# The high weight of ffn1 meets both parts of the rows in three matmuls of 364, 362 and 362 columns instead of four of 272

## The reference

```python
h2 = _rmsnorm(x, P['norm_ffn'])
gt, up = jnp.split(h2 @ P['w_ffn_in'], 2, axis=-1)
x = x + ((jax.nn.silu(gt) * up) @ P['w_ffn_out']).astype(x.dtype)
```

## Time and profile before

| | |
|---|---|
| median of three runs | 3008.64 us (3006.72 to 3013.38) |
| profiled execution, span from first to last instruction | 3010.2 us |
| mean granted TensorE clock | 0.954 of full |
| PE busy / PEld busy | 2699.9 us (90%) / 2534.6 us (84%) |
| POOL, DVE, ACT busy | 1315.4, 1119.3, 665.0 us |
| matmuls (and as many weight loads) | 25812 |
| ffn1 with dense matmuls, each of the two layers | about 257.5 us |

### The profile page before, as it was taken

One profiled execution on the slowest core, in us unless ns is written; L12 is line 12 of the kernel. 1 busy time (PEld: TensorE's weight loads), 2 busy tenths in 40 slices (PEclk: granted clock), 3 DMA queues, 4 the chain that ended last, 5 costly groups with the idle time before them and its releaser, 6 DMA issues.

```text
span 3010.2 us, 66079 instructions
## 1 busy us (share of the span) xinstructions
PE 2699.9 (90%) x25812; PEld 2534.6 (84%) x25812; DVE 1119.3 (37%) x1758; ACT 665.0 (22%) x1156; POOL 1315.4 (44%) x1083
## 2 busy tenths in 40 slices
PE   5898988889899989999978889888889999899997
PEld 5887877777799989999977778777878999899997
DVE  4435254462411231115644552535534113211165
ACT  3223232232211121111232232313222111211122
POOL 4333242431365545555542422414324555455564
PEclk9999999999699999999989999999988999999998
DMA  5112021110122323222321111202011223232122
GB/s 174 40 48 64 20 75 41 41 54 25 60 84 84 102 82 91 85 75 73 101 91 35 56 50 35 77 23 70 26 45 65 84 84 119 69 91 84 62 80 84
DMA packets 70704, 206.66 MB, mean 69 GB/s; under 512 B 10640, under 2 KB 14752, under 8 KB 69488
## 3 DMA queue, kind: packets, MB, share of 16 engines
q1 hardware_dynamic: 59760, 175.03, 18.9%
q10 hardware_dynamic: 7200, 16.26, 1.4%
q0 software_dynamic: 3552, 12.56, 1.3%
HBM read 185.20 MB, written 18.61 MB: 68 GB/s over the span
## 4 chain that ended last, share of the span: by engine, by line
PE 64%; DVE 13%; PEld 11%; issue 5%; ACT 2%; POOL 2%; DMA 2%; DVEq 0%; SPq 0%; ACTq 0%; PEldq 0%; POOLq 0%
PE psP L591 31%; PE psQ L591 13%; PE psQ L654 9%; PEld psP L591 8%; DVE BIG L1365 7%; PEld psQ L591 3%; PE psQ L647 3%; PE psQ L930 1%; DVE BIG L1368 1%; POOL WS L453 1%; PE psP L920 1%; DMA BIG<-in_s_ret 1%; DVE UB L1365 1%; PE psP L654 1%; PE psP L914 1%
## 5 line engine op out<-in xcount | busy, mean ns | idle before, releaser
L591 PE MATMUL psP<-HH,WS 128*128 128x272 f32 x5728 | 1074.2, 299 | 60.5 <-DVE HL L1365 19.9
L591 PEld LDWEIGHTS psP<-HH,WS 128*128 128x128 f32 x5728 | 852.3, 193 | 93.9 <-issue 24.9
L451 POOL TENSOR_SCALAR WS<-W 128x512 fp32r<-128x512 f32 (+1 forms) x312 | 246.0, 788 | 1145.3 <-PEq L585 712.7
L453 POOL TENSOR_TENSOR WS<-W,WS 128x512 fp32r<-128x512 f32 (+1 forms) x312 | 508.8, 1631 | 26.0
L591 PE MATMUL psP<-HL,WS 128*128 128x272 f32 x1984 | 417.8, 293 | 0.0
L654 PE MATMUL psQ<-BIG 64*64 64x64 f32 (+1 forms) x5696 | 283.9, 235 | 60.9 <-DVE BIG L1365 25.2
L591 PE MATMUL psQ<-BIGR 128*128 128x272 f32 x2032 | 333.3, 287 | 0.0
L591 PEld LDWEIGHTS psP<-HL,WS 128*128 128x128 f32 x1984 | 320.1, 193 | 0.0
L654 PEld LDWEIGHTS psQ<-BIG 64*64 64x64 f32 x5696 | 223.2, 135 | 111.8 <-issue 95.5
L591 PE MATMUL psQ<-HH,BIGR 128*128 128x272 f32 x1760 | 304.5, 287 | 0.0
L453 POOL TENSOR_TENSOR BIGR<-W,BIGR 128x512 fp32r<-128x512 f32 (+1 forms) x160 | 293.1, 1832 | 13.4
(11 more groups left out here) (226 smaller groups left out, 3047.9 us busy)
## 6 DMA issues: line engine op xcount, KB each, us to landing
W<-in_w_stage SPq DMA_DIRECT2D x88, 512.0 KB, 3.6
W<-in_w_f SPq DMA_DIRECT2D x88, 512.0 KB, 3.6
W<-in_w_gate SPq DMA_DIRECT2D x48, 512.0 KB, 3.6
W<-in_w_f SPq DMA_DIRECT2D x88, 256.0 KB, 2.6
W<-in_w_br SPq DMA_DIRECT2D x48, 256.0 KB, 2.6
W<-in_w_out SPq DMA_DIRECT2D x16, 512.0 KB, 3.6
x_waiting<-X SPq DMA_DIRECT2D x4, 1088.0 KB, 8.0
X<-x_waiting ACTq DMA_DIRECT2D x2, 2176.0 KB, 9.9
```

The costliest lines, as they stand in the source:

```text
L451: pool.tensor_scalar(high, src, 1.0, 0.0, ALU.mult, ALU.add).then_inc(high_part[q], 1)
L453: pool.tensor_tensor(low, src, high, ALU.subtract).then_inc(split[q], 1)
L591: mm = pe.matmul(out[:, a, 0:HT], a_, x_[:, a * HT:(a + 1) * HT], start=(first and n == 0), stop=(last and n == 2))
```

## The change

Rows for ffn1 get a layout of their own, `H2`: 1088 columns for each of the 8 input blocks, high and low part side by side. Columns 0 to 363 are the 272 high columns of the first half and 92 low ones; columns 364 to 725 are the 272 high columns of the second half and 90 low ones; columns 726 to 1087 are the other 362 low ones. The high weight runs over the 1088 columns in three matmuls (364, 362, 362), and the low weight over the two groups of 272 high columns in two: 40 matmuls for a tile instead of 48.

A gate tile now uses P0 (two banks) and a bank of Q0, an up tile P1 and a bank of Q1. The low columns' products no longer add up in PSUM under the high ones: ScalarE copies them out of three places into a buffer (`low_part`, three ACTIVATEs), VectorE adds the PSUM's high part to it (`join`), and sigmoid and products work on that sum. VectorE writes the low rows of norm2 in four pieces instead of one (`low_wide`), and ScalarE's high rows go into two groups of 272. `H2` lies where `HL` and a free block before it lie; `HH` is not read by ffn1 any more. After ffn1 ScalarE waits until the last product is written (`f_done`).

Three semaphores of two recurrent branches become one each, with counted values; two helpers of VectorE become names for the engine's own calls. Neither changes an instruction that computes.

```diff
+W1, W2 = 364, 362
...
-    ("ffn1", FF_T // 2, [("g0", "P0"), ("u0", "Q0"), ("g1", "P1"), ("u1", "Q1")]),
+    ("ffn1", FF_T, [("g", "P0"), ("u", "P1")]),
...
                 def ffn1(i, first):
                     for t in range(2):
-                        project_split(l, "ffn1", i, f"g{t}", HH, HL, rows=ROWS["H2"] if first and t == 0 else None)
-                        project_split(l, "ffn1", i, f"u{t}", HH, HL)
...
+                        for n in "gu":
+                            use = f"{n}{t}"
+                            b = wait_free(pe, l, "ffn1", 2 * i + t, n)
+                            third = ps["Q0" if n == "g" else "Q1"][:, 0]
+                            q = weights_split(l, "ffn1", i, use)
+                            for k in range(KD):
+                                if first and t == 0 and n == "g":
+                                    pe.wait_ge(rows_split, l * ROWS_N + ROWS["H2"] + k + 1)
+                                high, low = (v[:, k * P:(k + 1) * P] for v in SW[q])
+                                pe.matmul(b[:, 0, 0:W1], high, H2[:, k, 0:W1], start=k == 0, stop=False, skip_group_check=True)
+                                pe.matmul(b[:, 1, 0:W2], high, H2[:, k, W1:W1 + W2], start=k == 0, stop=False,
+                                          skip_group_check=True)
+                                pe.matmul(third[:, 0:W2], high, H2[:, k, W1 + W2:2 * TOK], start=k == 0, stop=k == KD - 1)
+                                pe.matmul(b[:, 0, 0:HT], low, H2[:, k, 0:HT], start=False, stop=k == KD - 1, skip_group_check=True)
+                                mm = pe.matmul(b[:, 1, 0:HT], low, H2[:, k, W1:W1 + HT], start=False, stop=k == KD - 1,
+                                               skip_group_check=True)
+                                release()
+                            mm.then_inc(fullof("ffn1", n), 1)
...
+                def low_part(dst, b, third):
+
+                    act.activation(dst[:, 0:W2], third[:, 0:W2], ACT.Copy)
+                    act.activation(dst[:, W2:W2 + W1 - HT], b[:, 0, HT:W1], ACT.Copy)
+                    return act.activation(dst[:, W2 + W1 - HT:TOK], b[:, 1, HT:W2], ACT.Copy)
+
                 with act.Fori(0, FF_T // 2) as i:
                     for t in range(2):
...
+                        b = wait_full(act, l, "ffn1", n, "g")
+                        act.wait_ge(f_done, l * FF_T + n + 1)
+                        low_part(NT[t], b, ps["Q0"][:, 0]).then_inc(f_low, 1)
+                        wait_emptied(act, l, "ffn1", n, "g")
+                        act.activation(SQ[t], NT[t], ACT.Sigmoid).then_inc(f_sig, 1)
+                        b = wait_full(act, l, "ffn1", n, "u")
+                        act.wait_ge(f_gated, l * FF_T + n + 1)
+                        low_part(NT[t], b, ps["Q1"][:, 0]).then_inc(f_low, 1)
+
+                act.wait_ge(f_done, l * FF_T + FF_T + 2)
...
+            def low_wide(l, n, k, src):
+
+                dve.wait_ge(rows_high, l * ROWS_N + n + 1)
+                v = H2[:, k]
+                tt(v[:, W1 + W2:W1 + W2 + HT], src[:, 0:HT], v[:, 0:HT], ALU.subtract)
+                tt(v[:, W1 + W2 + HT:2 * TOK], src[:, HT:W2], v[:, W1:W1 + W2 - HT], ALU.subtract)
+                tt(v[:, HT:W1], src[:, W2:W1 + W2 - HT], v[:, W1 + W2 - HT:W1 + W1 + W2 - 2 * HT], ALU.subtract)
+                tt(v[:, W1 + HT:W1 + W2], src[:, W1 + W2 - HT:TOK], v[:, W1 + W1 + W2 - 2 * HT:W1 + HT],
+                   ALU.subtract).then_inc(rows_split, 1)
...
                 with dve.Fori(0, FF_T // 2) as i:
                     for t in range(2):
...
+                        b = wait_full(dve, l, "ffn1", n, "g")
+                        dve.wait_ge(f_low, 2 * (l * FF_T + n) + 1)
+                        join(NT[t], b).then_inc(emptyof("ffn1", "g"), 1)
+                        dve.wait_ge(f_sig, l * FF_T + n + 1)
+                        wait_emptied(dve, l, "ffn1", n, "g")
+                        tt(SQ[t], SQ[t], NT[t], ALU.mult).then_inc(f_gated, 1)
+                        b = wait_full(dve, l, "ffn1", n, "u")
+                        dve.wait_ge(f_low, 2 * (l * FF_T + n) + 2)
+                        join(NT[t], b).then_inc(emptyof("ffn1", "u"), 1)
+                        wait_emptied(dve, l, "ffn1", n, "u")
+                        tt(FF[:, bass.ds(n, 1)], SQ[t].unsqueeze(1), NT[t].unsqueeze(1), ALU.mult).then_inc(f_done, 1)
+                        dve.wait_ge(f_done, l * FF_T + n + 3)
```

More of the change, by code:

```diff
@@ L150 @@
  sdec um vm A_sq A_rstd A_n A_y2 A_o
- B_g B_c0 B_c1 B_q B_k B_qd B_vm B_s1_ B_s2_ B_s3_ B_sq B_rstd B_n B_o
- C_g C_f0 C_f C_k0 C_qp C_tot C_vm C_s1_ C_s2_ C_s3_ C_dk C_sq C_rstd C_n C_o C_lvl C_add""".split()
+ B_g B_c0 B_c1 B_q B_k B_qd B_vm B_s B_sq B_rstd B_n B_o
+ C_g C_f0 C_f C_k0 C_qp C_tot C_vm C_s C_dk C_sq C_rstd C_n C_o C_lvl C_add""".split()
 def trunk(nc, A, OUT, XD):
@@ L283, in trunk @@
         M = blocks(BIG[:, 2 * ON:2 * ON + KD * TOK], TOK)
+        H2 = blocks(BIGR[:, at_r[0]:at_r[0] + 2 * KD * TOK], 2 * TOK)
         at_r[0] += KD * TOK
@@ L321, in trunk @@
         x_ready, f_sig = sem("x_updated"), sem("f_sigmoid")
+        f_low, f_gated, f_done = sem("f_low_part"), sem("f_gated"), sem("f_done")
         out_sems = {n: sem("st_" + n) for n in OUT}
@@ L1024, in ffn1 @@
                     for t in range(2):
-                        project_split(l, "ffn1", i, f"g{t}", HH, HL, rows=ROWS["H2"] if first and t == 0 else None)
-                        project_split(l, "ffn1", i, f"u{t}", HH, HL)
-                loop(FF_T // 2, ffn1)
+                        for n in "gu":
[16 more added lines that the diff above has]
+                            mm.then_inc(fullof("ffn1", n), 1)
+                            unreleased.append((l, "ffn1", 2 * i + t, n, split_used[q]))
+                ffn1(0, True)
+                unreleased.pop()
+                pe.sem_inc(go, 1)
+                with pe.Fori(1, FF_T // 2) as i:
+                    unreleased.append((l, "ffn1", 2 * i - 1, "u", split_used[SPLIT_TURNS.place("ffn1", "u1")]))
+                    ffn1(i, False)
+                    unreleased.pop()
+                unreleased.append((l, "ffn1", FF_T - 1, "u", split_used[SPLIT_TURNS.place("ffn1", "u1")]))
+                release()
                 pe.sem_inc(go, 1)
@@ L1103, in high, with high_h @@
                 act.activation(v, src, ACT.Copy).then_inc(rows_high, 1)
-            def high_h(n):
+            def high_h(n, wide=False):
                 for k in range(KD):
                     act.wait_ge(h_ready, n * KD + k + 1)
-                    high(HH[:, k], NT[k % 2])
+                    if wide:
+                        high(blocks(H2[:, k, 0:2 * W1], W1)[:, :, 0:HT], halves(NT[k % 2]))
+                    else:
+                        high(HH[:, k], NT[k % 2])
             with act.Fori(0, DEPTH) as l:
@@ L1322, in _ @@
                 norm(l, "norm2")
-                high_h(2 * l + 1)
+                high_h(2 * l + 1, wide=True)
+                def low_part(dst, b, third):
+                    act.activation(dst[:, 0:W2], third[:, 0:W2], ACT.Copy)
+                    act.activation(dst[:, W2:W2 + W1 - HT], b[:, 0, HT:W1], ACT.Copy)
+                    return act.activation(dst[:, W2 + W1 - HT:TOK], b[:, 1, HT:W2], ACT.Copy)
                 with act.Fori(0, FF_T // 2) as i:
                     for t in range(2):
[L1326 to L1332, removed]
+                        n = 2 * i + t
+                        b = wait_full(act, l, "ffn1", n, "g")
[7 more added lines that the diff above has]
+                act.wait_ge(f_done, l * FF_T + FF_T + 2)
                 def high_rows(half, i):
@@ L1361, in _ @@
             dve.sem_inc(x_ready, X_READY)
+            dve.sem_inc(f_done, 2)
             dve.sem_inc(sq_used, 2)
[L1364 to L1368, removed]
+            tt, stt = dve.tensor_tensor, dve.scalar_tensor_tensor
             steps = [0]
@@ L1421, in low_part @@
                         dve.wait_ge(x_stored[k // 4], stored)
-                    low(l, rows + k, parts[:, k], NT[k % 2], HH[:, k])
+                    if parts is None:
+                        low_wide(l, rows + k, k, NT[k % 2])
+                    else:
+                        low(l, rows + k, parts[:, k], NT[k % 2], HH[:, k])
                 for k in range(KD):
@@ L1633, in states @@
                             if c:
-                                w(S[f"{n}_s{c}_"])
+                                dve.wait_ge(S[f"{n}_s"], it * 3 + c)
                                 ins = stt(SS[n][:, c], SS[n][:, c - 1], decay(c), kv, ALU.mult, ALU.add)
@@ L1637, in states @@
                                 ins = dve.tensor_copy(SS[n][:, 0], kv)
-                            ins.then_inc(S[f"{n}_s{c + 1}_"] if c < 3 else emptyof(ph, f"{n}_kv"), 1)
+                            ins.then_inc(S[f"{n}_s"] if c < 3 else emptyof(ph, f"{n}_kv"), 1)
                     def level(n):
@@ L1774, in _, with join @@
```

(7 more changed lines are left out.)

## The result

The changed kernel takes 3025.69 us (five runs, 3019.62 to 3034.29) against 3008.64 us before: ratio 1.0058, 95% interval 1.0037 to 1.0079, that is 11 to 24 us slower. The forecast was no change, 3012.9 us, with 2994 to 3021 as range.

What follows compares the result with a forecast made beforehand. PE's matmul pace was taken to bound ffn1, ScalarE and VectorE its ends. Terms 3.6 + 3.6 + 4.0 + 1.0 - 7.9 = 4.3 us more than the profiled 3010.2 us, 3012.9 us on the median's side; range 2994 to 3021.

Steps and rivals of the forecast that it cites:

- The pace: ffn1's dense matmuls: one fewer per step saves a fixed 11.5 ns over 688 steps, 7.9 us in all.
- The third rival: ffn1: new column-group starts and a third PSUM bank slow wide matmuls a few ns each, eating the gain; chance 0.04.
- The row that I leaned on: float32 matmuls of 512 columns follow 0.43 us apart, 3 ns over the columns; taken as evidence for a fixed cost.
- the case: ffn1: the 11.5 ns above one clock per column are a fixed cost of each matmul; chance 0.55.
- The slower rival: ffn1: the 11.5 ns belong to the columns, a step stays 748.8 ns, total 3020.8 us; chance 0.13.
- The weight-load rival: ffn1: the load beside each matmul sets the pace, a step takes 711.9 ns, gain 25.4 us, total 2995.4; chance 0.22.
- Low parts: norm2 on VectorE: four subtractions instead of one add 0.22 us per block, 3.6 us over two layers.
- The clock behind it: PE after norm2: slower blocks may keep half clock up to 3.9 us; 0.5 us taken per layer, 0 to 2.0.
- The end of ffn1: Between ffn1 and ffn2: copies, join and contended product add 1.8 us per layer, 3.6 in all.
- The clock behind the pause: Start of ffn2: half clock after a 4.8 us PE idle gap; 2.0 us per layer, 4.0 in all (0 to 5.5).
- The cover: ffn1: copies and join free a gate tile's PSUM after about 1.7 us, within one up tile's 5.9, so PE never waits.
- the signs: Expected in the trace: 5.90 us tiles, norm2 blocks 1.67 us apart, PE idle 4.8 us before ffn2, clock 0.5 behind it.

Runs made afterwards that it cites:

- the last kernel: Kernel before with its six matmuls and short drain, but ffn1's rows in a buffer of their own and ffn2's first rows split early: 3009.64 us.
- The pace kernel: Kernel before with ffn1 gate tiles in 512-column matmuls and up tiles with weights of 64 columns; 230.9 ns per 512-column matmul, 124.4 ns per 272-column one.
- the first experiment: Changed kernel with six matmuls of 272 columns per step instead of 364, 362, 362, 272, 272: 3029.92 us, ratio 1.0073.
- the filler: Changed kernel with 36 unused matmuls of 272 columns added on TensorE in the pause between ffn1 and ffn2: 3020.78 us, ratio 1.0042.
- the old drain: Changed kernel with PSUM drained as before, without copies and joins, the low rows' sums left out: 3020.67 us, ratio 1.0040.
- the low columns in a row: Changed kernel with columns ordered 272 high, 544 low, 272 high, in matmuls of 368, 352, 368, and one low subtraction: 3017.59 us, ratio 1.0028.

## Why the prediction was wrong

**The pace** is the step that failed most. The sum had 688 x 11.5 ns = 7.9 us, on two grounds: that the 11.5 ns above one clock per column belong to the matmul, and that moving the rows changes nothing else in the stream. The runs show 5.1 ns a step and 3.3 to 3.5 us, made up of two things. With the rows in the new place in both kernels, five matmuls instead of six save 9.3 ns a step (752.7 to 743.4), some 6.4 us. The new place itself costs 3.8 to 4.2 ns a step (748.5 to 752.3 and 752.7), some 2.6 to 2.9 us, and the sum had nothing for it. The third rival, at 0.04, had an effect of this kind, but gave it to the starting columns of the groups and to a third PSUM bank. Groups at multiples of 16 columns leave the average as it is, and the last kernel has no third bank and the slow pace all the same. Why the place of the rows costs time stays open.

How the 11.5 ns divide between a matmul and its columns is open too. The pace kernel gives 4.6 ns to the matmul in the layout of before, the first experiment 9.3 in that of the change. Both are less than 11.5, and tiles of one kernel differ by up to 16 ns a step with the same shapes. The row that I leaned on, float32 matmuls of 512 columns, was a stream that feeds each column twice; I noted that it was not a proof and gave the case 0.55 all the same. The slower rival, that all 11.5 ns belong to the columns, had 0.13 and a time, 3020.8 us, that the first interval contains. That agreement is luck: its step of 748.8 ns was not measured, and the half clocks below make up for it. The weight-load rival fell with the weights of 64 columns, and with 230.9 ns at 512 columns where it had 216.

The Trainium skill ("TensorE: Matmul & The Clock Gate", Back-to-back issue gap) gives about 2.5 ns above the columns. By it the gain would be 1.7 us, nearer to the 3.3 to 3.5 measured than my 7.9. The trace does not agree with the rule itself: what lies above the columns is 11.5 ns at 272 columns and 17.6 at 512.

**norm2.** Low parts: 1.8 us per layer forecast, 1.65 measured (last low part 18.40 us after norm2's sum, 16.75 before). The clock behind it was mis-sized: 0.5 us taken, 0 to 2.0 as bounds. It stayed at half for 3.4 us, by my estimate some 1.2 us of loss (with 1.45 us a block these stretches are 2.9 us shorter, and 1.65 of that is the low parts); the two together show as +2.4 us to the first up tile and some 0.5 in the tiles after it.

**The end of ffn1.** 1.8 us forecast, 1.88 measured; copies, join and contended product came as worked out.

**The clock behind the pause.** 2.0 us taken, 2.75 the upper bound from the stretch ahead of the output projection; measured 2.8 and 2.7 with the filler, and 3.8 and 2.8 us for all of ffn2. The upper bound was the better value.

**The cover** held: PE has no idle time between ffn1 tiles, and the pace with the old drain is the same. So did most of the signs: a tile takes 5.95 us, within 5.8 to 6.0, blocks of norm2 come 1.66 us apart, PE waits 4.86 us ahead of ffn2 and the clock behind that is 0.5. The waits and pauses came as described; what failed is the term of the pace and the size of the two clocks.

Per layer the forecast was -3.95 + 1.8 + 0.5 + 1.8 + 2.0 = +2.15 us (pace, low parts, clock at norm2, end of ffn1, clock behind it); the traces give -1.63 + 1.65 + 1.2 + 1.88 + 2.75 = +5.9 against +6.9 and +5.9 in the table. The pace takes 2.3 of the 3.7 us per layer that were missing, the two clocks 1.45. Beyond the 12.8 us of both layers the profile has 2.0 us, and the medians a few more, in the untouched part; no experiment settles that.

## What to carry to other kernels

Before fewer, wider matmuls are bought, measure the old matmuls in the new layout, and the new widths in it: here the layout took back almost half of what the widths gave, and one width in one layout could show neither. Price a pause of TensorE with the clock behind it, and take the dearer of the nearest rows. A change whose own gain is small may still open something, here a row buffer that ffn1 no longer reads: rows split early were worth more than the widths.

## What was not expected of the hardware

Six matmuls of the same shape took 748.5 ns or 752.3 to 752.7 ns a step depending on where their rows lie. In the changed kernel the step was 747 ns in gate tiles and 740 in up tiles (mean of starts over 1130 to 1330 us), and 752 and 736 with the low columns in a row. With the kind of tile both the weights' buffers and the PSUM banks alternate, and no experiment separates the two.

The product of two SBUF operands, hidden in ffn1, took 2.63 us on average, not 0.72, beside POOL's splitting. The join of as many columns, with one operand in PSUM, took 0.72 us beside the same splitting (groups of VectorE, count, busy us, mean ns):

```profile
L1831 DVE TENSOR_TENSOR UB<-UB,psP 128x544 f32<-128x544 f32 x88 | 63.5, 721 | 232.4 <-ACT UB L1361 232.4
L1846 DVE TENSOR_TENSOR BIG<-UC,UB 128x544 f32 x44 | 115.9, 2633 | 6.7 <-DVE UB L1831 3.8
```

A pause of 2.98 us left the clock alone in the kernel before and halved it for 3.4 us in the kernel with the old drain, in both layers each.
